# Block products with seven instead of eight multiplications for eight of w_down's 22 tiles

## The chip, the cores and the metric

One core of a Trainium2 chip runs the whole kernel. The metric is device microseconds from launch to end; the median of three runs stands for a kernel. Times below are microseconds (us) unless marked ns. Engines: PE is TensorE, DVE is VectorE, ACT is ScalarE, POOL is GpSimd, SP is SyncE, whose queue issues the loads.

## The reference, cut to what matters

One encoder layer over 512 prompt tokens and 32 sample tokens, 544 in all, with model width 1024 (8 tiles of 128) and hidden width 2816 (22 tiles of 128). It has two feed-forward steps with weights of their own, one ahead of the token mixer and one behind it:

```
g, u = split(rms_norm(r) @ w_gate_up)        # 1024 -> 2 x 2816
h    = silu(g) * u                           # 544 tokens x 2816
y    = h @ w_down                            # 2816 -> 1024
r    = r + 0.5 * rms_norm(y)
```

Behind the first come the mixer (projection, windowed attention and short convolution, projection), behind the second a gate stage ("ple") that ends the layer. All matrices are fp32.

## The kernel before

Every operand of a matmul is split into a high and a low part, `hi` (a rounded copy made by ACT) and `lo` (the rest, source minus hi, made by DVE). A product of two tiles is then three matmuls: hi x hi, hi x lo, lo x hi. Tokens are on the free axis in two halves A and B of 272 (`HT`), so one matmul is 128x128 weights times 128x272. Weights come by SP's queue into four slots of `raw`, are split into `w_split`, and are used.

The stages run in the order up1, down1, mix, out, up2, down2, ple.

**up.** The first `NCL` = 5 hidden tiles are plain products. The other `NJ` = 17 are done in "jobs" of seven block products (the Strassen-Winograd scheme, 2x2 blocks: two halves of the 8 input tiles, gate and up columns, two token halves). A block product is four tiles times three matmuls, 12 matmuls, and a job 84. The order is written out by hand in `SEVEN`: products 1, 2, (3 of the job before), 6, (4 of the job before), 7, 5. In a job DVE makes the block sums (`first_sums`, L1334), POOL two more (L685, L687), ACT the hi parts (`block_hi`, L800), DVE the lo parts (`block_lo`, L1349), and ACT and DVE combine the results (`keep_p1`, `job_c11`, and so on). The split blocks of even and odd jobs have a buffer each.

**down.** `down_group` makes four groups of two output tiles. A group is 2 output tiles x 2 token halves x 22 hidden tiles x 3 matmuls. ACT takes each result out of PSUM (`evacuate`: a square for the norm, then a copy into `y_down`). The hidden tiles are split into `h_hi` and `h_lo` as the last job of up ends (`hidden_hi`, `hidden_lo`). The last group is `last_group`: while PE works on half B, half A's sum of squares (added up by POOL, summed over partitions by a ones-matmul, `all_sums`) is turned into a scale, DVE scales and adds to the residual (`chain_r`), ACT and DVE make the next stage's input (`chain`, `chain_lo`), and the next stage's weights are split (`split_hi`, `split_lo`).

Each engine runs its instructions in the order in which the program issues them; a semaphore wait holds all that is behind it on that engine. At the start of mix, PE asks for the sum of half B's squares (SUM0+2) before the second pair of units (L2178); in ple it asks for it at the seventh of eight input tiles of the first pair:

```
{2: lambda: all_sums(n2 + 1), 6: lambda: all_sums(n2 + 2)}
```

## Time and profile before

| | |
|---|---|
| median of 3 runs | 1053.0 us (1052.49 to 1053.06) |
| span of the profiled execution, first to last instruction | 1051.1 us |
| that execution's own time | not listed; the median is 1.9 us above the span |
| mean granted TensorE clock | 0.996 of full |
| down1 on PE | 260.1 to 393.3 us |
| down2 on PE | 832.3 to 966.6 us |

The times come from the row groups further down. A row of a timeline has the start, the length, the engine and line, output and inputs, how many instructions it merges, and in brackets the idle time before it with what ended it. A matmul's length includes its passage through the array; the next one starts well before it ends, so time per matmul is read from a stretch and its count, not from a length.

### The profile page before, as it was taken

Reading aid. Unit: us, or ns where it says so; the run is one execution under the profiler, and the core shown is the slowest. Engines: PE = TensorE matmul, PEld = TensorE weight load, DVE = VectorE, ACT = ScalarE, POOL = GpSimd, SP = SyncE. Lnnn points to the kernel's source line nnn. Section 1 sums busy time; section 2 is a strip of 40 time slices with the busy share of each in tenths; the row PEclk is TensorE's granted clock in tenths of the full one; section 3 lists DMA queues with packets and bytes.
Section 4 is the critical chain, followed back from the end, with each engine's and each line's share of the span. In section 5 each row is a group of like instructions: output and inputs, shape, how many; then the busy total and the mean of one; then the engine's idle time right before and its main releaser. Section 6 shows DMA issues by size and latency. Waiting matters only on the chain.

```text
span 1051.1 us, 20152 instructions
## 1 busy us (share of the span) xinstructions
PE 1032.0 (98%) x8115; PEld 1015.1 (97%) x8115; DVE 696.1 (66%) x1055; ACT 509.5 (48%) x931; POOL 266.0 (25%) x208
## 2 busy tenths in 40 slices
PE   7999999999999999999999999999999999999997
PEld 7999999999999999998999999999999999999897
DVE  5889777777512259678695898977777741127843
ACT  5555555555522254434455645555555631126664
POOL 3112443431211133000323201343434021113221
PEclk9999999999999999999999999999999999999999
DMA  8314342425333304231224121443333542233102
GB/s 238 94 41 112 91 119 81 121 80 139 102 92 110 80 1 86 80 88 51 70 82 122 41 81 52 112 119 92 110 86 103 147 115 71 83 100 90 34 1 86
DMA packets 182679, 94.77 MB, mean 90 GB/s; under 512 B 11768, under 2 KB 180928, under 8 KB 182592
## 3 DMA queue, kind: packets, MB, share of 16 engines
q1 hardware_dynamic: 182576, 93.56, 32.2%
q8 instruction: 61, 1.00, 0.4%
q14 instruction: 26, 0.21, 0.1%
q10 hardware_dynamic: 16, 0.00, 0.0%
HBM read 91.15 MB, written 2.50 MB: 89 GB/s over the span
## 4 chain that ended last, share of the span: by engine, by line
PE 85%; DVE 9%; ACT 2%; issue 1%; POOL 1%; DMA 1%; SPq 1%; POOLq 0%; DVEq 0%; ACTq 0%
PE bank L1837 14%; PE bank L1835 14%; PE bank L1836 14%; PE bank L1964 9%; PE bank L1967 9%; PE bank L1966 9%; PE bank L1884 5%; PE bank L1892 2%; PE misc L2045 2%; PE misc L1964 1%; PE misc L1967 1%; PE misc L1966 1%; DVE w_split L1242 1%; DVE x_lo L1272 1%; DVE rpre L1248 1%
## 5 line engine op out<-in xcount | busy, mean ns | idle before, releaser
L1837 PE MATMUL bank<-h_hi,w_split 128*128 128x272 f32 x704 | 203.9, 290 | 0.0
L1835 PE MATMUL bank<-h_hi,w_split 128*128 128x272 f32 x704 | 203.0, 288 | 0.0
L1836 PE MATMUL bank<-h_lo,w_split 128*128 128x272 f32 x704 | 202.2, 287 | 0.0
L1242 DVE TENSOR_TENSOR w_split<-raw,w_split 128x1408 fp32r<-128x1408 f32 (+2 forms) x66 | 98.0, 1496 | 146.1 <-ACT w_split L740 146.1
L653 POOL TENSOR_TENSOR ssq<-ssq,sq 128x272 f32<-128x272 f32 x99 | 96.6, 975 | 220.0 <-ACT sq L745 214.3
L1836 PEld LDWEIGHTS bank<-h_lo,w_split 128*128 128x128 f32 x704 | 132.7, 188 | 0.1
L1835 PEld LDWEIGHTS bank<-h_hi,w_split 128*128 128x128 f32 x704 | 132.4, 188 | 0.1
L1837 PEld LDWEIGHTS bank<-h_hi,w_split 128*128 128x128 f32 x704 | 132.3, 188 | 0.0
L1964 PE MATMUL bank<-t_hi,even_blocks 128*128 128x272 f32 x432 | 125.3, 290 | 0.6 <-DVE tU L1367 0.5
L1967 PE MATMUL bank<-t_hi,even_blocks 128*128 128x272 f32 x432 | 125.0, 289 | 0.0
L1966 PE MATMUL bank<-t_lo,even_blocks 128*128 128x272 f32 x432 | 124.4, 288 | 0.0
L740 ACT ACTIVATE w_split<-raw 128x1408 fp32r<-128x1408 f32 (+2 forms) x66 | 80.7, 1242 | 80.7 <-PE bank L1837 74.7
L685 POOL TENSOR_TENSOR s_rest<-s,raw_up 128x512 f32<-128x512 f32 x30 | 66.2, 2207 | 207.6 <-DVE s L1334 207.6
L1964 PE MATMUL bank<-t_hi,odd_blocks 128*128 128x272 f32 x384 | 111.6, 291 | 1.0 <-ACT kept L815 0.8
L1967 PE MATMUL bank<-t_hi,odd_blocks 128*128 128x272 f32 x384 | 111.1, 289 | 0.0
L1966 PE MATMUL bank<-t_lo,odd_blocks 128*128 128x272 f32 x384 | 110.5, 288 | 0.0
L1836 PE MATMUL bank<-x_lo,w_split 128*128 128x272 f32 x320 | 92.1, 288 | 0.0
L1964 PEld LDWEIGHTS bank<-t_hi,even_blocks 128*128 128x128 f32 x432 | 81.3, 188 | 0.9 <-issue 0.9
L1966 PEld LDWEIGHTS bank<-t_lo,even_blocks 128*128 128x128 f32 x432 | 81.4, 188 | 0.0
L1967 PEld LDWEIGHTS bank<-t_hi,even_blocks 128*128 128x128 f32 x432 | 81.3, 188 | 0.0
L1964 PEld LDWEIGHTS bank<-t_hi,odd_blocks 128*128 128x128 f32 x384 | 72.2, 188 | 1.8 <-issue 1.2
L1966 PEld LDWEIGHTS bank<-t_lo,odd_blocks 128*128 128x128 f32 x384 | 72.4, 189 | 0.0
(280 smaller groups left out, 2626.1 us busy)
## 6 DMA issues: line engine op xcount, KB each, us to landing
raw_up<-w_ffn_gate_up SPq DMA_DIRECT2D x88, 512.0 KB, 5.0
raw<-w_ffn_down SPq DMA_DIRECT2D x32, 704.0 KB, 4.8
raw<-w_in SPq DMA_DIRECT2D x14, 512.0 KB, 4.1
raw<-w_ple_gate SPq DMA_DIRECT2D x8, 512.0 KB, 3.8
x_tok<-x_prompt SPq DMA_DIRECT2D x4, 512.0 KB, 5.2
raw<-w_in SPq DMA_DIRECT2D x8, 256.0 KB, 3.8
raw<-w_out SPq DMA_DIRECT2D x16, 128.0 KB, 3.4
raw<-w_out SPq DMA_DIRECT2D x8, 256.0 KB, 3.8
```

What stands on the lines that cost most here:

```text
L653: nc.gpsimd.tensor_tensor(dst, dst, sq[:, s % 2, :], ALU.add).then_inc(summed, 1)
L685: nc.gpsimd.tensor_tensor(s24(j)[:, 0, :], s31[:, 1, :], a[:, 0, :], ALU.add).then_inc(s24_made[n], 1)
L740: nc.scalar.activation(chunk_part(c, 0), chunk_raw(c), ACT.Copy).then_inc(hi_made, 1)
L1242: nc.vector.tensor_tensor(chunk_part(c, 1), chunk_raw(c), chunk_part(c, 0).bitcast(F32), ALU.subtract).then_inc(lo_made, 1)
L1835: nc.tensor.matmul(psum(u), wh, hi, start=(k == 0), stop=False)
L1836: nc.tensor.matmul(psum(u), wh, lo, start=False, stop=False)
L1837: mm = nc.tensor.matmul(psum(u), wl, hi, start=False, stop=(k == n - 1))
L1884: nc.tensor.matmul(psum(u), chunk_part(c, part)[:, k, :], high(k, h), start=(k == 0 and part == 0), stop=False)
L1892: mm = nc.tensor.matmul(psum(u), chunk_part(c, 0)[:, k, :], low(k, h), start=False, stop=(k == KD - 1))
L1964: nc.tensor.matmul(out, hi[:, k, :], x_h, start=(k == 0 and p in (1, 2, 7)), stop=False, skip_group_check=True)
L1966: nc.tensor.matmul(out, hi[:, k, :], x_l, start=False, stop=False, skip_group_check=True)
L1967: mm = nc.tensor.matmul(out, lo[:, k, :], x_h, start=False, stop=(k == 3), skip_group_check=True)
```

## The change

Both down stages are done in three pieces over the 22 hidden tiles.

1. Tiles 0 to 2 (`CA` = 3) by plain products, 16 results of 9 matmuls (`first_tiles`), through three PSUM banks. Their weights (3 tiles x 1024 columns) come in four loads of 384 KB behind product (NJ-2, 4) of the up stage. ACT copies each result to `y_part` (`first_copy`).
2. Tiles 3 to 10 in `NF` = 4 jobs of seven block products (`folded`), each job two output tiles wide, both token halves at once; the 2x2 blocks are two sets of four hidden tiles, two output tiles, two token halves. The token-side blocks are sums of hidden tiles (`fold_sum`, `fold_hi`, `fold_lo`), made once. DVE adds the products into `y_part`: seven adds of 128x272 a job.
3. Tiles 11 to 21 by plain products, 16 results of 33 matmuls; DVE adds `y_part` (`y_add`), then ACT squares from SBUF (`square_y`).

Around them, SP waits for the mixer's cache loads until all of half B's residual is done, the loops of down are written out, and the hidden tiles are split for both halves at once (`hidden_hi`, `hidden_lo`, groups of 3, 2, 2, 2, 2 tiles).

The order and SP's loads of the first tiles:

```diff
-    H_GROUPS = ((0, 2), (14, 18), (2, 4), (4, 6), (6, 10), (10, 14), (18, KF))
+    H_GROUPS = ((11, 14), (14, 16), (16, 18), (18, 20), (20, KF))
...
+    def seven_order(first, last):
+        order = [(j - late, p) for j in range(first, last)
+                 for p, late in ((1, 0), (2, 0), (3, 1), (6, 0), (4, 1), (7, 0), (5, 0)) if j - late >= first]
+        return order[:-2] + [(last - 1, p) for p in (5, 7, 3, 4)]
+    SEVEN, FOLDED = seven_order(0, NJ), seven_order(FOLD0, FOLD0 + NF)
...
+            def load_first_tiles(n, s):
+                sp.wait_ge(product_done[n], nth(NJ - 2, 4))
+                for part in range(4):
+                    cols = slice(part * D // 4, (part + 1) * D // 4)
+                    sp.dma_start(ca_raw[:, :, cols], w_down[s][0:CA * P, cols].rearrange("(k p) c -> p k c", p=P))\
+                        .then_inc(ca_in[part], 16)
```

On ACT, the first tiles, the fold jobs and the squares:

```diff
+            def first_copy(n, v):
+                act.wait_ge(ca_done, 2 * KD * n + v + 1)
+                nc.scalar.activation(y_part(v // 2, v % 2), ca_bank(v), ACT.Copy).then_inc(ca_copied, 1)
...
+            def fold_jobs(n, s, d):
+                after = {0: lambda: first_weights_hi(n, 2), 1: lambda: fold_hi(n, 3), 2: lambda: first_weights_hi(n, 3),
+                         3: lambda: fold_hi(n, 4), 4: lambda: block_hi(n, s, FOLD0, 0), 5: lambda: fold_hi(n, 5),
+                         6: lambda: block_hi(n, s, FOLD0, 1), 8: lambda: fold_hi(n, 6),
+                         10: lambda: block_hi(n, s, FOLD0, 2), 12: lambda: block_hi(n, s, FOLD0, 3)}
+                for v in range(2 * KD):
+                    first_copy(n, v)
+                    if v in after:
+                        after[v]()
+                for j in range(FOLD0 + 1, FOLD0 + NF):
+                    for m in range(4):
+                        block_hi(n, s, j, m)
+                    if j == FOLD0 + 1:
+                        hidden_hi(n, 0)
+                hidden_hi(n, 1)
+                hidden_hi(n, 2)
+                hidden_hi(n, 3)
+                split_hi(C0[d])
                 split_hi(C0[d] + 1)
-                hidden_hi(n, A, 4)
-                job_gate_b(n, NJ - 1)
-            def hidden_hi(n, h, g):
+                hidden_hi(n, 4)
...
+            def square_y(s, i, h, pos):
+                act.wait_ge(y_ready, Y0[s] + 8 * i + 4 * h + pos + 1)
+                square(y_sum(4 * i + pos, h), SQ0[s] + (4 * h if i == 0 else 8 + (4 + KD) * h) + pos).then_inc(squared, 1)
```

On DVE, an add into `y_part`, the end of the up jobs, the fold jobs, and the last output tiles:

```diff
+            def add_p1(n, j):
+                m, i = 2 * (j - FOLD0), j - FOLD0
+                dve.wait_ge(product_done[n], nth(j, 1))
+                dve.wait_ge(ca_copied, 2 * KD * n + 2 * KD)
+                if i:
+                    dve.wait_ge(c11_added, NF * n + i)
+                nc.vector.tensor_tensor(p1_kept_at, chain_bank(j), y_part(m, A), ALU.add).then_inc(p1_added, 1)
...
+                j = NJ - 1
+                job_c22(n, j - 1)
+                job_c11(n, j)
+                fold_sum(n, 1)
+                job_c21(n, j - 1)
+                job_hidden(n, j - 1)
+                job_c22(n, j)
+                first_tiles_lo(n, 1, CA)
+                first_weights_lo(n, 0)
+                fold_sum(n, 2)
+                first_sums(n, s, FOLD0)
+                first_weights_lo(n, 1)
+                job_c21(n, j)
+                job_hidden(n, j)
+                first_weights_lo(n, 2)
+                fold_sum(n, 3)
+                first_weights_lo(n, 3)
+                fold_lo(n, 0), fold_lo(n, 1)
+                block_lo(n, s, FOLD0, 0)
+                fold_lo(n, 2)
+                block_lo(n, s, FOLD0, 1)
+                fold_lo(n, 3)
+                block_lo(n, s, FOLD0, 2), block_lo(n, s, FOLD0, 3)
+                fold_lo(n, 4)
...
+            def fold_jobs(n, s, d):
+                for j in range(FOLD0, FOLD0 + NF - 1):
+                    if j > FOLD0:
+                        add_u4(n, j - 1)
+                        add_c22(n, j - 1)
+                    first_sums(n, s, j + 1)
+                    add_p1(n, j)
+                    block_lo(n, s, j + 1, 0)
+                    add_c11(n, j)
+                    if j > FOLD0:
+                        add_c12(n, j - 1)
+                    block_lo(n, s, j + 1, 1)
+                    add_u2(n, j)
+                    if j > FOLD0:
+                        add_c21(n, j - 1)
                     else:
+                        fold_lo(n, 5), fold_lo(n, 6)
+                    block_lo(n, s, j + 1, 2)
+                    block_lo(n, s, j + 1, 3)
+                    if j > FOLD0:
+                        continue
+                    hidden_lo(n, 0)
+                j = FOLD0 + NF - 1
+                add_u4(n, j - 1)
+                add_c22(n, j - 1)
+                add_p1(n, j)
+                hidden_lo(n, 1)
+                add_c11(n, j)
+                add_c12(n, j - 1)
+                hidden_lo(n, 2)
+                add_u2(n, j)
+                add_c21(n, j - 1)
+                hidden_lo(n, 3)
+                add_u4(n, j)
+                split_lo(C0[d])
+                add_c22(n, j)
                 split_lo(C0[d] + 1)
+                add_c12(n, j)
+                add_c21(n, j)
+                hidden_lo(n, 4)
...
+            def y_add(s, i, h, pos):
+                n, v, m = FFN[s], 8 * i + 4 * h + pos, 4 * i + pos
+                if v == 0:
+                    for added in (c11_added, c12_added, c21_added, c22_added):
+                        dve.wait_ge(added, NF * (n + 1))
+                dve.wait_ge(unit_done, U0[s] + v + 1)
+                nc.vector.tensor_tensor(y_sum(m, h), psum(U0[s] + v), y_part(m, h), ALU.add).then_inc(y_ready, 1)
+            def down_stage(s, ci):
+                c0, c1, with_p = C0[s], C0[s] + KD, s == "down2"
+                split_lo(c0 + 2), split_lo(c0 + 3)
+                for pos in range(4):
+                    y_add(s, 0, A, pos)
+                for pos, j in enumerate((6, 7, 4, 5)):
+                    y_add(s, 0, B, pos)
+                    split_lo(c0 + j)
+                for pos in range(4):
+                    y_add(s, 1, A, pos)
+                chain_r(ci, A, y_sum, SUM0[s], {3: lambda: y_add(s, 1, B, 0), 6: lambda: y_add(s, 1, B, 1)})
+                split_lo(c1), split_lo(c1 + 1)
                 if with_p:
                     p_lo(0)
+                chain_lo(ci, A, range(0, KD // 2))
+                y_add(s, 1, B, 2)
+                split_lo(c1 + 2)
                 if with_p:
                     chain_lo(ci, A, range(KD // 2, KD))
                     p_lo(1), p_lo(2)
+                    y_add(s, 1, B, 3)
                 else:
+                    y_add(s, 1, B, 3)
+                    split_lo(c1 + 3)
                     chain_lo(ci, A, range(KD // 2, KD))
```

On PE, the first tiles and the waits of the fold jobs:

```diff
+            def first_tiles(n):
+                for v in range(2 * KD):
+                    m, h = divmod(v, 2)
+                    if v == 0:
+                        pe.wait_ge(ca_lo_made, 2 * n + 2)
+                    if v % 4 == 0:
+                        pe.wait_ge(ca_w_lo_made, 4 * n + v // 4 + 1)
+                    if v > 2:
+                        pe.wait_ge(ca_copied, 2 * KD * n + v - 2)
+                    cols = slice(m * P, (m + 1) * P)
+                    for k in range(CA):
+                        x_h, x_l = half(ca_hi, k, h), half(h_lo, k, h)
+                        nc.tensor.matmul(ca_bank(v), ca_w_hi[:, k, cols], x_h, start=(k == 0), stop=False)
+                        nc.tensor.matmul(ca_bank(v), ca_w_hi[:, k, cols], x_l, start=False, stop=False)
+                        mm = nc.tensor.matmul(ca_bank(v), ca_w_lo[:, k, cols], x_h, start=False, stop=(k == CA - 1))
+                    mm.then_inc(ca_done, 1)
...
+                    if p == 6:
+                        pe.wait_ge(p1_added, NF * n + i + 1)
+                    if p == 5:
+                        pe.wait_ge(u2_added, NF * n + i + 1)
+                    if p == 3:
+                        pe.wait_ge(u4_added, NF * n + i + 1)
...
+                    if p == 4:
+                        pe.wait_ge(c22_added, NF * n + i + 1)
```

## Rows read from the trace of the kernel before

**Rows 1.** The page: busy time by engine; granted clock in 40 slices.

```profile
PE 1032.0 (98%) x8115; PEld 1015.1 (97%) x8115; DVE 696.1 (66%) x1055; ACT 509.5 (48%) x931; POOL 266.0 (25%) x208
...
PEclk9999999999999999999999999999999999999999
```

**Rows 2.** Windows (busy by engine, clock, DMA): jobs of up1, down1.

```profile
78.70:260.10 181.40, 180.86 (x1431) 180.26 (x1430) 140.46 (x162) 96.94 (x156) 65.43 (x30) 1.00 0.38 105
260.10:393.30 133.20, 133.20 (x1061) 133.12 (x1060) 47.21 (x46) 47.44 (x74) 26.82 (x23) 1.00 0.29 81
```

**Rows 3.** Costliest groups: one of down's three matmul lines.

```profile
L1837 PE MATMUL bank<-h_hi,w_split 128*128 128x272 f32 x704 | 203.9, 290 | 0.0
```

**Rows 4.** Waits of PE, whole span: waiter, releaser, total, times, longest.

```profile
PE bank L1884 <- ACT x_hi_up L758: 3.1, 1, 3.1
...
PE misc L2045 <- ACT out_tok L1192: 1.5, 1, 1.5
...
PE bank L1964 <- DVE tU L1367: 0.5, 1, 0.5
```

**Rows 5.** DVE groups by shape, 78 to 394 us: busy, mean, idle before.

```profile
L1334 DVE TENSOR_TENSOR s<-raw_up 128x1024 f32<-128x1024 f32 x16 | 19.5, 1216 | 0.0
...
L1427 DVE TENSOR_TENSOR h_lo<-h_raw,h_hi 128x1088 fp32r<-128x1088 f32 x8 | 10.1, 1290 | 0.9 <-ACT h_hi L885 0.9
...
L1349 DVE TENSOR_TENSOR even_blocks<-s_rest,even_blocks 128x1024 fp32r<-128x1024 f32 x8 | 9.8, 1219 | 0.5 <-ACT even_blocks L800 0.5
...
L1349 DVE TENSOR_TENSOR even_blocks<-raw_up,even_blocks 128x512 fp32r<-128x512 f32 x9 | 6.2, 685 | 0.0
...
L1367 DVE TENSOR_TENSOR tU<-bank,kept 128x272 f32<-128x272 f32 x9 | 4.0, 439 | 2.9 <-ACT kept L822 2.9
```

**Rows 6.** ACT groups by shape, the same stretch.

```profile
L885 ACT ACTIVATE h_hi<-h_raw 128x1088 fp32r<-128x1088 f32 x8 | 8.6, 1106 | 2.4 <-PE bank L1967 1.5 <-DVE h_raw L1382 1.0
...
L815 ACT ACTIVATE kept<-bank 128x272 f32<-128x272 f32 x17 | 6.8, 397 | 17.3 <-PE bank L1967 17.3
```

**Rows 7.** Timeline of DVE, then POOL, in one up1 job (start, length).

```profile
239.22 1.97 DVE L1349 TENSOR_TENSOR even_blocks<-s,even_blocks 128x1024 fp32r<-128x1024 f32 x1
...
243.31 0.44 DVE L1374 TENSOR_TENSOR tU<-bank,kept 128x272 f32<-128x272 f32 x1 [2.12 <-PE bank L1967]
...
237.89 2.21 POOL L685 TENSOR_TENSOR s_rest<-s,raw_up 128x512 f32<-128x512 f32 x1 [6.15 <-DVE s L1334]
```

**Rows 8.** Window in which three loads of w_down arrive.

```profile
248.00:250.00 2.00, 2.00 (x18) 2.00 (x17) 0.64 (x2) 0.95 (x3) 0.00 (x0) 1.00 1.02 302
```

**Rows 9.** Timeline at the end of down1: DVE, PE, PE.

```profile
388.85 3.51 DVE L1242 TENSOR_TENSOR w_split<-raw,w_split 128x1024 fp32r<-128x1024 f32 x2
...
397.30 1.08 PE L1857 MATMUL misc<-ssq,ones 128*128 128x272 f32 x4
...
409.44 4.53 PE L1884 MATMUL bank<-x_hi_a,w_split 128*128 128x272 f32 x34 [0.66 <-DVE zq L1603]
```

**Rows 10.** Timeline of POOL there: one squares add.

```profile
376.95 0.77 POOL L653 TENSOR_TENSOR ssq<-ssq,sq 128x272 f32<-128x272 f32 x1 [7.55 <-ACT sq L745]
```

**Rows 11.** Timeline at the end of down2: three of DVE, two of PE.

```profile
965.23 2.78 DVE L1272 SCALAR_TENSOR_TENSOR x_lo<-r,gT,x_hi_a 128x272 fp32r<-128x272 f32 x4
...
971.50 1.41 DVE L1503 TENSOR_TENSOR pT_lo<-misc,pT_hi 128x272 fp32r<-128x272 f32 x4
...
976.81 1.86 DVE L1248 RECIPROCAL misc<-misc 128x272 f32<-128x272 f32 x1
...
970.14 0.70 PE L1857 MATMUL misc<-ssq,ones 128*128 128x272 f32 x2
...
984.86 2.77 PE L1884 MATMUL bank<-x_hi_a,w_split 128*128 128x272 f32 x20 [0.26 <-DVE tG L1770]
```

**Rows 12.** PE's timeline, then a window, at the start of the kernel.

```profile
12.50 5.82 PE L1884 MATMUL bank<-x_hi_up,w_up 128*128 128x272 f32 x32 [3.07 <-ACT x_hi_up L758]
...
13.00:14.00 1.00, 1.00 (x7) 1.00 (x6) 1.00 (x3) 1.00 (x4) 0.00 (x0) 0.50 1.22 288
```

More of the change, by code:

```diff
@@ L57, in encoder_layer @@
     NJ = KF - NCL
-    STAGES = [("up1", 2 * KF, 4 * NCL, KD), ("down1", 2 * KD, 2 * KD, MAXK), ("mix", len(MIX), 2 * len(MIX), KD),
-              ("out", KD, 2 * KD, KD), ("up2", 2 * KF, 4 * NCL, KD), ("down2", 2 * KD, 2 * KD, MAXK),
+    CA, NF = 3, KD // 2
+    FOLD0, NJT = NJ + 1, NJ + NF
+    STAGES = [("up1", 2 * KF, 4 * NCL, KD), ("fold1", KD, 0, KD), ("down1", KD, 2 * KD, MAXK),
+              ("mix", len(MIX), 2 * len(MIX), KD), ("out", KD, 2 * KD, KD), ("up2", 2 * KF, 4 * NCL, KD),
+              ("fold2", KD, 0, KD), ("down2", KD, 2 * KD, MAXK),
               ("ple", KD, 4 * KD, KD + KP)]
@@ L127, in encoder_layer @@
              ("norm_ffn2_post", "norm_ple_pre"), ("norm_ple_post", None)]
-    FFN = {"up1": 0, "down1": 0, "up2": 1, "down2": 1}
+    FFN = {"up1": 0, "fold1": 0, "down1": 0, "up2": 1, "fold2": 1, "down2": 1}
+    FOLD = {"up1": "fold1", "up2": "fold2"}
     SQ0 = {"start": 0, "down1": 16, "mix": 48, "out": 64, "down2": 96, "ple": 128}
@@ L407, in encoder_layer @@
               for s, w in (("up1", "w_ffn1_gate_up"), ("up2", "w_ffn2_gate_up"))}
-        down = {s: t[w][0].rearrange("(j k p) (m c) -> m j p k c", j=2, p=P, c=P)
-                for s, w in (("down1", "w_ffn1_down"), ("down2", "w_ffn2_down"))}
+        w_down = {"up1": t["w_ffn1_down"][0], "up2": t["w_ffn2_down"][0]}
+        fold = {s: w[CA * P:(CA + 8) * P, :].rearrange("(k p) (m c) -> m p k c", p=P, c=P) for s, w in w_down.items()}
+        down = {s: w[(CA + 8) * P:FF, :].rearrange("(k p) (m c) -> m p k c", p=P, c=P) for s, w in w_down.items()}
         w_in = t["w_in"][0].rearrange("(k p) n -> p k n", p=P)
@@ L583, in _ @@
             sp.dma_start(x_tok[0:DEC, XT - 1, :], t["x_sample"][0]).then_inc(x_in[XT - 1], 16)
-            for s, d in (("up1", "down1"), ("up2", "down2")):
+            for n, (s, d) in enumerate((("up1", "down1"), ("up2", "down2"))):
                 load_up(s, 2 if s == "up1" else 0, SLOTS)
@@ L862, in jobs @@
                         keep_u4(n, j)
[L863 to L886 removed]
+                    block_hi(n, s, j + 1, 2)
@@ L1383, in job_hidden, with first_tiles_lo, first_weights_lo @@
                                         up_at(j)[:].rearrange("p h t -> p (h t)"), ALU.mult).then_inc(h_job_made[n], 1)
-            def jobs(n, s, d):
-                for j in range(NJ):
-                    more = j + 1 < NJ
+            def first_tiles_lo(n, a, b):
+                dve.wait_ge(ca_hi_made, 2 * n + (2 if a else 1))
+                nc.vector.tensor_tensor(h_lo[:, a:b], h_raw[:, a:b], ca_hi[:, a:b].bitcast(F32), ALU.subtract)\
+                    .then_inc(ca_lo_made, 1)
+            def first_weights_lo(n, part):
+                cols = slice(part * D // 4, (part + 1) * D // 4)
+                dve.wait_ge(ca_w_hi_made, 4 * n + part + 1)
+                nc.vector.tensor_tensor(ca_w_lo[:, :, cols], ca_raw[:, :, cols], ca_w_hi[:, :, cols].bitcast(F32),
+                                        ALU.subtract).then_inc(ca_w_lo_made, 1)
@@ L1389, in jobs, with fold_lo @@
+            def fold_lo(n, b):
+                dve.wait_ge(fold_hi_made, 7 * n + b + 1)
+                if b == 2:
+                    dve.wait_ge(fold_summed, 4 * n + 4)
+                nc.vector.tensor_tensor(fold_low(b), fold_raw(b), t_hi[:, b].bitcast(F32), ALU.subtract)\
+                    .then_inc(fold_lo_made, 1)
+            def jobs(n, s):
+                for j in range(NJ - 1):
                     if j > 1:
                         job_c22(n, j - 1)
-                    if more:
-                        first_sums(n, s, j + 1)
+                    first_sums(n, s, j + 1)
@@ new lines, in down_stage @@
+            def down_stage(s, n, hooks_b):
+                first_tiles(n)
+                folded(n)
+                for v in range(2 * KD):
+                    i, h, pos = v // 8, v % 8 // 4, v % 4
+                    c, hooks = C0[s] + 4 * i + pos, hooks_b.get(pos) if (i, h) == (1, B) else None
+                    if h == A:
+                        pe.wait_ge(lo_made, split_no[c])
+                    if v < 4:
+                        pe.wait_ge(c12_added if v < 2 else c21_added, NF * n + NF - 1 + v % 2)
+                    else:
+                        pe.wait_ge(y_ready, Y0[s] + v - 3)
+                    if v == 0:
+                        hooks = {a - MAXK: lambda g=g: pe.wait_ge(h_lo_made[n], g + 1) for g, (a, _) in enumerate(H_GROUPS)}
+                    product(U0[s] + v, [(c, k - MAXK, h_high(k, h), half(h_lo, k, h)) for k in range(MAXK, KF)], hooks)
```

467 lines of the change are left out of this document (267 added, 200 removed).

## The prediction

> **What bounds the kernel now.** I read the page first: PE is busy for 98% of the span, DVE for 66%, at a granted clock of nine tenths or more throughout [rows 1]. So a matmul that is taken away shortens the kernel, unless another engine makes PE wait in its place. Next the windows: 1061 matmuls in the 133.20 us of down1 is 0.126 us each, and the 17 jobs of up1 (17 x 84 = 1428 matmuls in 181.4 us) come to 0.127 [rows 2]. I use 0.126, which makes a block product (12 matmuls) 1.51 us. Last the waits of PE: hardly any lie in the stages that change; the long ones are 3.1 us at the start of the kernel and 1.5 us in ple [rows 4]. The timelines at the two ends of down show something the shares hide: there DVE, not PE, sets when the next stage can go on. PE waits 0.66 us on DVE at 409.44 and again at 984.86 [rows 9, 11].
>
> **The matmuls.** Before, each of down's three matmul lines has 704 in both stages [rows 3], 2112 in all, 1056 a stage. After: 16 x 9 = 144, 4 x 84 = 336, 16 x 33 = 528, together 1008. That is 48 fewer a stage, 96 in all: 96 x 0.126 = **-12.1 us**. Everything else is a matter of waits.
>
> **Entry to the first tiles.** PE's 0.5 us wait on `job_c22` in up2's last job [rows 4] goes, since that add is no longer behind a split: **-0.5**. New is the wait for the first tiles' weights. Their loads start when product (15, 4) ends, four products or 6.0 us before PE wants them. With three loads on the way the DMA moves 302 GB/s [rows 8], so 0.39 MB is 1.3 us, behind a start-up that I put at 2 to 2.5 us. Then come ACT's copy of 768 elements (about 0.8, between 0.40 for 272 and 1.11 for 1088 [rows 6]) and DVE's difference (about 0.95, between 0.69 for 512 and 1.22 for 1024 [rows 5]). 3.6 + 0.8 + 0.95 = 5.4 fits in 6.0. I take **+0.2** for both stages; if landing takes 5 us it is +1 each.
>
> **The 18.1 us of first tiles.** A result is 9 x 0.126 = 1.13 us and PE may be two results ahead of ACT's copies. Up to the eighth copy ACT has 8 x about 0.33 plus seven larger operations of 0.75 to 1.0 us (ends overlap the next start, so I take a little off the lengths of [rows 6]): about 9.1 us, started 1.6 us into the stage, done at 10.7. PE needs that copy for its eleventh result, at 11.3. So 0, and up to +0.7 a stage. DVE has about 17.5 us of work between the first weights' lo part and the last `fold_lo` (eight operations of 1088 elements at 1.20, three weight parts at 0.9, the block sums and lo parts at 1.14, 1.14, 1.14, 1.14 and 0.65, two adds), and ends about when PE does; the last one is not needed for another 6.0 us. 0.
>
> **The first fold job** has a place where DVE is late. It has only five products, 7.53 us, since products 3 and 4 belong to the next. Call its start on PE F. The first product ends at F + 1.7 with latency; from there DVE must do in order: `add_p1` 0.35, lo part 1.14, `add_c11` 0.35, the lo part beside POOL's sums 1.97, `add_u2` 0.35, two `fold_lo` 2.40, lo parts 1.14 and 0.65, `hidden_lo` of 1632 elements 1.80, `add_u4` 0.35: 10.5 us (lengths of [rows 5, 7], less the 0.08 by which successors overlap). `add_u4` is done at F + 12.2. PE asks for it at product (18, 3), the eighth: F + 7 x 1.507 = F + 10.55. Wait 1.7 us. Behind it DVE's `add_c22` 0.35, `first_sums` 1.14, `add_p1` 0.35 end at F + 14.1, while PE asks at F + 13.8: 0.35 more. After that DVE has an add of 0.35 in place of the 0.78 us hidden product and three adds more, some 0.7 us in a job in which it idles 2.1 us for one wait alone [rows 7]: no further wait. Two stages x 2.05 = **+4.1**. Bounds: 0.7 a stage if the 1.97 is 1.22 and the splits overlap better; 3.3 if the fold splits run into POOL's sums as that one does.
>
> The Trainium skill says in GPSIMD Engine Reference, section Specifications, that POOL and VectorE contend when a VectorE instruction has two SBUF inputs. The trace agrees in part: 1.97 us beside POOL's sum against 1.22 for the same shape without it, while other lo parts are not stretched [rows 5, 7]. If it held for each of them, the fold jobs' wait would be at the upper bound above.
>
> **The last fold job and the plain tiles.** Nothing is late there by the same sums: `add_c22` ends 0.35 us before product (21, 4), and `y_add` has 4.15 us a result. 0.
>
> **End of down1.** The results of half B are now added on DVE instead of copied by ACT, four adds of 0.36 in the queue where PE already waits. `chain_r` ends 0.72 later, 389.6 in the old time frame. Then two splits 3.5 [rows 9], `chain_lo` on four tiles 2.7, `y_add` (B, 2) 0.36, a split 1.14 to 1.75, `y_add` (B, 3) 0.36: about 398.0. ACT squares (0.4), POOL adds (0.77 [rows 10], up to 1.5 beside a split), so PE's sum of half B can run at 399.1 to 400.4. Before it ran from 397.30 [rows 9]. PE waits about 2.2 us. It gets 0.66 of this back at 409.44, where it waited anyway; DVE's own chain is 1.0 to 1.6 later. **+1.6**, between 1.0 and 2.8.
>
> **End of down2** is worse. DVE's queue was: `x_lo` from 965.23, a split, more `x_lo`, `pT_lo`, which ends at 972.9 [rows 11]. The two early adds are absorbed (DVE waited there for ACT), `y_add` (B, 2) costs 0.36, and `y_add` (B, 3) comes after all of them: 973.65. Square 0.4, POOL's add 0.8, latencies: 975.1. PE wants the sum at 970.14 [rows 11]: a wait of 5.0 us. Next the gates: two tiles of hi x hi and the lo pass, 2 us, give DVE gate 0 at 977.8 and gate 1 at 978.8; split 1.4, and the reciprocal that ran from 976.81 starts at 980.6, 3.8 late. PE itself is 5.0 late less 0.35 and 0.26 of old waits, so the matmuls of 984.86 start 4.4 late: **+4.4**, between 3.5 and 5.5.
>
> **The clock there.** At the start of the kernel PE waited 3.07 us, the granted clock fell to 0.50 (1.2 GHz), and the next 32 matmuls took 5.66 us to the next instruction instead of 4.0 [rows 12]. The 1.5 us wait of [rows 4] left it at 2.4 GHz [rows 1]. A wait of 5.0 us is nearer to the first: **+1.5** in down2's end, 0 elsewhere (2.2 is below 3.07); bounds 0 and 1.7 for each of the two ends. [...]
>
> **Sum.** -12.1 - 0.5 + 0.2 + 4.1 + 1.6 + 4.4 + 1.5 = -0.8 us. The span becomes 1051.1 - 0.8 = 1050.3; the median stands 1.9 above the span, so 1052.2; I round to **1052.0**.
>
> **Rivals.**
> - *The late adds cost less.* If PE reaches the two sums later, or the clock holds, the ends cost 3 us instead of 7.5 and the fold jobs 2 instead of 4.1: -12.1 - 0.5 + 0.2 + 2 + 3 = -7.4, 1045.6. For it: all terms but the matmuls rest on DVE's queue being as full as I count it. Against it: the chain of PE on DVE at both ends is in the trace. With a part of it (no clock loss and a better fold job, -3.5) it is 1049.5. Chance 0.35 together, most of it in the nearer part.
> - *DVE becomes the bound at the fold jobs.* If POOL's sums stretch each split beside them, the fold jobs wait 3.3 a stage (+2.5), the first tiles' copies 0.7 (+1.4), and the clock also falls at down1's end (+1.7): already the first is enough with one of the others; from +2.9 over my sum the kernel is slower. All of it gives 1057.8. For it: 1.97 against 1.22 [rows 7, 5]. Against: only one of four lo parts shows it. Chance 0.2.
> - *The weights of the first tiles are late.* +1 to +2 in all, 1053.5; inside no change. It has 0.1 of the chance below.
>
> My forecast with the third rival has the remaining 0.45. 0.2% is 2.1 us, about what a measurement of this kernel can tell: faster is below 1050.9, slower above 1055.1. From the cases: faster 0.36, same 0.44, slower 0.20. The range reaches to the nearer part of the first rival and to the start of the second: 1047.5 to 1055.5.
>
> **What would show it.** PE with 96 matmuls fewer; a wait of about 1.7 us in each fold stage at the eighth product, ended by DVE's add for product 5; a wait of about 2 us ahead of the sums at the start of mix; one of about 5 us at the last sum of half B in ple, released by POOL behind ACT behind DVE, and after it a window with a clock near 0.5. If PE shows no such wait in ple, my order of DVE's queue is wrong and the time is that of the first rival. If ACT is named as the releaser between the first tiles, the copies are late and it is the second.

## The result, and the profile after

| | before | after |
|---|---|---|
| median | 1053.03 us (20 runs) | 1054.64 us (20 runs, 1053.55 to 1055.29) |
| ratio | | 1.0014, 95% interval 1.0007 to 1.002 |
| span of the profiled execution | 1051.1 us | 1051.8 us |
| mean granted clock | 0.996 | 0.994 |
| down1 starts on PE | 260.1 us | 259.7 us |
| mix starts | 393.3 us | 390.2 us |
| wait on `zq` in mix ends | 409.4 us | 407.5 us |
| down2 starts | 832.2 us | 829.5 us |
| ple starts | 966.6 us | 961.3 us |
| output transposes start | 992.9 us | 993.6 us |

The change made the kernel slower by 0.14%: less than the 0.2% that I called no change, and inside the range, but 2.6 us above the forecast and on the other side of the kernel before: I had 1.0 us faster, it is 1.6 slower.

The page of the changed kernel, its first part. It answers to [rows 1]: 96 matmuls fewer, and DVE from 66% to 74%.

```profile
PE 1021.9 (97%) x8019; PEld 1003.8 (95%) x8019; DVE 782.3 (74%) x1183; ACT 532.0 (51%) x955; POOL 285.0 (27%) x224
```

The waits of PE over the whole span, as in [rows 4]: waiter, releaser, total, times, longest.

```profile
PE misc L2127 <- issue: 5.2, 1, 5.2
PE bank L2328 <- DVE kept L1626: 3.0, 2, 1.5
...
PE bank L2328 <- DVE kept L1620: 1.6, 2, 0.8
PE misc L2127 <- POOL ssq L739: 1.5, 1, 1.5
...
PE bank L2328 <- DVE kept L1607: 0.6, 2, 0.3
```

L2127 is `all_sums`: 5.2 us at the last sum of half B in ple, 1.5 at the same sum in mix. L1626 is `add_u4`, L1620 `add_u2`, L1607 `add_p1`, once in each down stage. The waits for `add_u4`, `add_p1` and the two sums are in the prediction, with 1.7, 0.35, 5.0 and 2.2 us. The one for `add_u2` is not. The wait on `tU` (0.5) is gone, as forecast.

TensorE's timeline across the first fold job of down1 (start, length, what it waited for). The first product starts at 277.72.

```profile
283.62 0.29 PE L2331 MATMUL bank<-t_hi,even_blocks 128*128 128x272 f32 x1
284.70 0.36 PE L2328 MATMUL bank<-t_hi,even_blocks 128*128 128x272 f32 x1 [0.80 <-DVE kept L1620]
284.90 0.29 PE L2330 MATMUL bank<-h_lo,even_blocks 128*128 128x272 f32 x1
...
289.16 0.29 PE L2331 MATMUL misc<-t_hi,odd_blocks 128*128 128x272 f32 x1
290.96 0.36 PE L2328 MATMUL bank<-t_hi,even_blocks 128*128 128x272 f32 x1 [1.51 <-DVE kept L1626]
...
292.42 0.29 PE L2331 MATMUL bank<-t_hi,even_blocks 128*128 128x272 f32 x1
292.99 0.36 PE L2328 MATMUL bank<-t_hi,odd_blocks 128*128 128x272 f32 x1 [0.28 <-DVE kept L1607]
```

The starts tell more than the bracket. In a run of matmuls they are 0.126 us apart. Over the three waits they are 1.08, 1.80 and 0.57 apart, and the start behind each is 0.20 further on, not 0.126. So waits listed with 0.80 + 1.51 + 0.28 = 2.6 us cost TensorE's stream of matmuls 0.95 + 1.67 + 0.44 + 3 x 0.07 = 3.3 us. The stage as a whole says the same: 133.2 us before, 130.5 after, and 48 matmuls are 6.05, so 3.4 us went elsewhere. The second stage gives 134.4 and 131.8, 3.4 again.

DVE's timeline in that job, then POOL's. They answer to [rows 7].

```profile
278.31 1.21 DVE L1456 TENSOR_TENSOR s<-raw_up 128x1024 f32<-128x1024 f32 x1
279.44 0.42 DVE L1607 TENSOR_TENSOR kept<-bank,y_low 128x272 f32<-128x272 f32 x1
279.79 2.17 DVE L1471 TENSOR_TENSOR odd_blocks<-raw_up,odd_blocks 128x1024 fp32r<-128x1024 f32 x1
281.89 0.43 DVE L1614 TENSOR_TENSOR y_low<-misc,kept 128x272 f32<-128x272 f32 x1
282.24 1.96 DVE L1471 TENSOR_TENSOR odd_blocks<-s,odd_blocks 128x1024 fp32r<-128x1024 f32 x1
284.13 0.43 DVE L1620 TENSOR_TENSOR kept<-bank,y_low 128x272 f32<-128x272 f32 x1
```

```profile
279.59 1.29 POOL L766 TENSOR_TENSOR s_rest<-s,raw_up 128x512 f32<-128x512 f32 x1 [14.12 <-DVE s L1456]
280.97 2.15 POOL L768 TENSOR_TENSOR s_rest<-s_rest,raw_up 128x512 f32<-128x512 f32 x1
```

Two lo parts are stretched beside POOL's sums, not one: 2.17 and 1.96 against 1.21 alone. And POOL's first sum is the quick one here, 1.29, where it took 2.21 in [rows 7].

The ends of these rows show how the two engines share the time: they take turns. POOL's first sum ends at 280.88, and the lo part that started during it ends 1.08 later, at 281.96. POOL's second sum started during that lo part and ends 1.16 after it, at 283.12. The second lo part started during that sum and ends 1.08 after it, at 284.20. So 2.17, 2.15 and 1.96 are each a wait for the other engine's instruction and then the operation's own time.

The end of down2: PE, then DVE, then windows (length; busy time and count of PE, PEld, DVE, ACT, POOL; granted clock; DMA share; GB/s). They answer to [rows 11, 12].

```profile
970.21 1.24 PE L2127 MATMUL misc<-ssq,ones 128*128 128x272 f32 x2 [5.23 <-issue]
970.87 2.40 PE L2154 MATMUL bank<-x_hi_b,w_split 128*128 128x272 f32 x8
```

```profile
967.07 1.40 DVE L1767 TENSOR_TENSOR pT_lo<-misc,pT_hi 128x272 fp32r<-128x272 f32 x4
968.39 0.42 DVE L1777 TENSOR_TENSOR y_down<-bank,y_high 128x272 f32<-128x272 f32 x1
```

```profile
968.00:970.20 2.20, 0.00 (x0) 0.02 (x1) 1.35 (x4) 0.78 (x2) 0.76 (x1) 0.50 0.23 63
...
972.20:973.20 1.00, 1.00 (x6) 1.00 (x6) 0.00 (x0) 1.00 (x1) 0.00 (x0) 0.50 0.00 0
...
974.20:975.20 1.00, 1.00 (x10) 1.00 (x9) 0.41 (x1) 0.00 (x0) 0.00 (x0) 1.00 0.00 0
```

`y_add` (B, 3), L1777, stands behind `pT_lo` and is done at 968.8. ACT's square and POOL's add follow it, and the sum runs at 970.21. The name "issue" in the row hides this chain: PE stood behind several semaphores, and the last is POOL's. While PE stands, the granted clock falls to 0.50, which is 1.2 GHz, and it is back at 1.00 (2.4 GHz) in the last window. What the low clock costs is read from the starts (a window's count also takes in matmuls that only reach into it): from the eight matmuls to the group behind them it is 2.20 us here (970.87 to 973.07). In the kernel before it was 1.21, 970.47 to 971.68, with this row:

```profile
970.47 1.37 PE L1884 MATMUL bank<-x_hi_b,w_split 128*128 128x272 f32 x8
```

### The profile page after: what moved, and what is told of

Read it like the earlier page. It is cut to its first block, busy times and chain, and to the rows that moved or that the text cites. A ratio compares the mean times of both kernels' runs of the same rounds, so it can differ in the third digit from the quotient of the medians.

```text
span 1051.8 us, 20086 instructions
## 1 busy us (share of the span) xinstructions
PE 1021.9 (97%) x8019; PEld 1003.8 (95%) x8019; DVE 782.3 (74%) x1183; ACT 532.0 (51%) x955; POOL 285.0 (27%) x224
## 4 chain that ended last, share of the span: by engine, by line
PE 85%; DVE 10%; issue 2%; ACT 1%; DMA 1%; SPq 1%; POOL 0%; POOLq 0%; DVEq 0%; ACTq 0%
PE bank L2105 11%; PE bank L2106 11%; PE bank L2107 11%; PE bank L2234 9%; PE bank L2236 9%; PE bank L2237 9%; PE bank L2154 5%; PE bank L2162 2%; PE bank L2328 2%; PE bank L2331 2%; PE bank L2330 2%; PE misc L2352 2%; PE misc L2236 1%; PE misc L2234 1%; PE misc L2237 1%
## 5 line engine op out<-in xcount | busy, mean ns | idle before, releaser
L766 POOL TENSOR_TENSOR s_rest<-s,raw_up 128x512 f32<-128x512 f32 x38 | 77.9, 2049 | 304.9 <-DVE s L1456 304.9
L739 POOL TENSOR_TENSOR ssq<-ssq,sq 128x272 f32<-128x272 f32 x99 | 93.0, 939 | 127.0 <-ACT sq L828 121.4
L768 POOL TENSOR_TENSOR s_rest<-s_rest,raw_up 128x512 f32<-128x512 f32 x38 | 80.9, 2130 | 3.0
L1364 DVE TENSOR_TENSOR w_split<-raw,w_split 128x1024 fp32r<-128x1024 f32 (+2 forms) x46 | 66.2, 1455 | 16.6 <-ACT w_split L823 16.6
L2106 PE MATMUL bank<-h_lo,w_split 128*128 128x272 f32 x264 | 76.1, 288 | 0.0
L2234 PEld LDWEIGHTS bank<-t_hi,odd_blocks 128*128 128x128 f32 x384 | 72.3, 188 | 1.7 <-issue 1.1
L2237 PEld LDWEIGHTS bank<-t_hi,odd_blocks 128*128 128x128 f32 x384 | 72.3, 188 | 0.0
L823 ACT ACTIVATE w_split<-raw 128x1024 fp32r<-128x1024 f32 (+2 forms) x46 | 53.1, 1181 | 37.7 <-PE bank L2107 29.1
L2105 PE MATMUL bank<-x_hi_a,w_split 128*128 128x272 f32 x240 | 70.7, 294 | 0.6 <-DVE w_split L1364 0.6
L2107 PE MATMUL bank<-x_hi_a,w_split 128*128 128x272 f32 x240 | 69.2, 288 | 0.0
L2106 PEld LDWEIGHTS bank<-x_lo,w_split 128*128 128x128 f32 x320 | 60.3, 188 | 0.0
```

The lines of the kernel that those rows point to most:

```text
L739: nc.gpsimd.tensor_tensor(dst, dst, sq[:, s % 2, :], ALU.add).then_inc(summed, 1)
L766: nc.gpsimd.tensor_tensor(s24(j)[:, 0, :], s31[:, 1, :], a[:, 0, :], ALU.add).then_inc(s24_made[n], 1)
L768: nc.gpsimd.tensor_tensor(s24(j)[:, 1, :], s24(j)[:, 0, :], a[:, 1, :], ALU.add).then_inc(s24_made[n], 1)
L823: nc.scalar.activation(chunk_part(c, 0), chunk_raw(c), ACT.Copy).then_inc(hi_made, 1)
L1364: nc.vector.tensor_tensor(chunk_part(c, 1), chunk_raw(c), chunk_part(c, 0).bitcast(F32), ALU.subtract).then_inc(lo_made, 1)
L2105: nc.tensor.matmul(psum(u), wh, hi, start=(k == 0), stop=False)
```

## The experiments

All times are medians; the changed kernel is 1054.6, the kernel before 1053.0 (1052.9 to 1053.05 in its executions beside the experiments). The own time of a profiled execution is 1.74 to 1.84 us above its span wherever it is on record.

### 1. The last add ahead of the lo parts (ple_add_early)

```
 if with_p:
-    chain_lo(ci, A, range(KD // 2, KD))
-    p_lo(1), p_lo(2)
     y_add(s, 1, B, 3)
+    chain_lo(ci, A, range(KD // 2, KD))
+    p_lo(1), p_lo(2)
```

> Against the changed kernel (1054.6): the last y_add of down2 stands right behind the split of the third weight tile, ahead of the rest of x_lo and pT_lo. Theory (DVE's queue order makes PE wait 5.2 us for the last sum in ple, and the idle time costs the clock about 1.5 us more): the wait falls to 1 to 1.5 us, the granted clock stays at full after it, and the time falls by 4.5 to 6 us, to 1049 to 1050. Rival (the sum is held by POOL's backlog or by ACT, not by DVE's order): the wait stays above 4 us and the time moves by less than 1 us. Rival (DVE's own chain ends last anyway, so PE's wait is hidden): the wait goes but comes back at PE's next wait on DVE, and the time moves by less than 2 us.

Measured: 1049.7 us, ratio 0.9968 (0.9956 to 0.998); 4.9 us less than the changed kernel. PE's timeline in ple, then windows:

```profile
967.48 0.70 PE L2127 MATMUL misc<-ssq,ones 128*128 128x272 f32 x2 [2.05 <-issue]
967.81 1.37 PE L2154 MATMUL bank<-x_hi_b,w_split 128*128 128x272 f32 x8
969.02 2.14 PE L2162 MATMUL bank<-x_lo,w_split 128*128 128x272 f32 x16
```

```profile
966.00:968.00 2.00, 0.52 (x3) 0.49 (x3) 2.00 (x4) 0.60 (x2) 1.10 (x2) 1.00 0.61 177
```

The wait is 3.2 us shorter (I had expected 1 to 1.5 us to be left; 2.05 are), the clock stays at 1.00, and the eight matmuls take 1.37 us instead of 2.40. From the start of ple to the output transposes it is 27.7 us, 4.5 less than in the changed kernel and 1.4 more than in the kernel before. So the order of DVE's queue is most of what the end of down2 costs.

### 2. The mixer's last sum later (mix_sum_late)

```
-second={0: lambda: (all_sums(n0 + 1), all_sums(n0 + 2))}
+second={0: lambda: all_sums(n0 + 1), 6: lambda: all_sums(n0 + 2)}
```

> Against the changed kernel (1054.6): PE asks for half B's sum in mix six tiles later. Theory (behind down1 DVE's chain sets the start of half B's matmuls, so PE's 1.5 us wait in front of the sum is only in the place of a later one): the 1.5 us wait goes, the wait on DVE near 407.5 grows from 0.66 to about 2 us, and the time changes by less than 0.5 us. Rival (PE's wait is a loss by itself): 1.2 to 1.5 us faster.

Measured: 1054.47 us, ratio 1.001 (1.0001 to 1.0019): 0.2 less than the changed kernel, within its scatter. The waits of PE in mix are now:

```profile
396.81 3.04 PE L2154 MATMUL bank<-x_hi_a,w_split 128*128 128x272 f32 x22 [0.66 <-DVE w_split L1364]
406.83 1.30 PE L2154 MATMUL bank<-x_hi_a,w_split 128*128 128x272 f32 x6 [0.29 <-ACT x_hi_a L841]
408.79 3.40 PE L2154 MATMUL bank<-x_hi_a,w_split 128*128 128x272 f32 x25 [0.65 <-DVE zq L1873]
```

The 1.5 us wait on POOL is gone. The wait on `zq` did not grow to 2 us, as I had expected; two smaller ones, on DVE and on ACT, stand ahead of it. The stretch from the start of mix to the end of the wait on `zq` is 17.55 us, against 17.35 in the changed kernel. So asking later for this sum gains nothing. That fits a chain through DVE that sets the time, with the wait at the start of mix as the first place where its lateness shows; no run made that chain earlier at this end.

### 3. The hidden chunk's lo part out of the first fold job (hidden_late)

```
-if j > FOLD0:
+if j < FOLD0 + 2:
     continue
 hidden_lo(n, 0)
```

> Against the changed kernel (1054.6): the first hidden_lo (1632 elements, 1.8 us) is moved from the end of DVE's first fold job to the end of the third. Theory (DVE is over-full only in the first fold job): PE's wait of 1.5 us on add_u4 and of 0.3 us on the next add_p1 go, the one of 0.8 us on add_u2 stays, and nothing new comes in the later jobs; 2 x 1.8 = 3.6 us faster, 1051.0. Rival (DVE is the bound through all fold jobs): the wait moves to a later fold job, less than 1 us faster.

Measured: 1050.92 us, ratio 0.998 (0.9971 to 0.9989); 3.7 less than the changed kernel. The waits of PE, whole span:

```profile
PE bank L2328 <- DVE kept L1620: 1.6, 2, 0.8
...
PE bank L2328 <- DVE kept L1607: 0.5, 2, 0.3
```

The wait for `add_u4` is gone in both stages and the two others are untouched. By the starts of the matmuls it was 1.67 + 0.07 us a stage, 3.5 in both, near the 3.7 measured. The 1.8 us of hidden work has room in the third fold job.

### 4. TensorE kept busy ahead of the sum in ple (ple_turns)

```
 def all_sums(n, size=None):
+    if n == SUM0["down2"] + 2:
+        pe.wait_ge(inverted, ...)
+        pe.wait_ge(p_ready, 1)
+        for _ in range(36):
+            nc.tensor.transpose(misc[:, 1, 384:512], ones[:], ident[:])
     pe.wait_ge(summed, SUMMED[n])
```

> Against the changed kernel (1054.6): PE makes 36 transposes of ones that nobody reads (about 4.6 us) in its wait for the last sum in ple, and nothing else changes. Theory (the wait also costs the clock): the sum comes at the same time, the granted clock stays at full behind it, and the time falls by about 1.5 us, to 1053.1. Rival (the clock is not what is lost, or DVE hides it): within 0.4 us of 1054.6.

Measured: 1052.41 us, ratio 0.9993 (0.9984 to 1.0002); 2.2 less than the changed kernel, though it does more. PE's timeline:

```profile
965.37 4.09 PE L2118 MATMUL misc<-ident,ones 128*128 128x128 f32 x36
970.72 0.73 PE L2132 MATMUL misc<-ssq,ones 128*128 128x272 f32 x2 [1.26 <-POOL ssq L739]
971.08 1.36 PE L2159 MATMUL bank<-x_hi_b,w_split 128*128 128x272 f32 x8
```

PE gets its sum no sooner, and now the releaser is named: POOL. The eight matmuls take 1.36 us, not 2.40. So the clock alone is worth about 2 us of the 6 at this end: 2.2 by the medians, and 1.8 by the traces, in which the stretch from the start of ple to the output transposes is 30.5 us instead of 32.2. My term for it was 1.5, with a bound of 1.7: the size was a little low.

### 5. The lo part ahead of `add_p1` (lo_before_p1)

```
 first_sums(n, s, j + 1)
-add_p1(n, j)
 block_lo(n, s, j + 1, 0)
+add_p1(n, j)
```

> Edit: in the fold jobs VectorE makes the first lo part of the next job's blocks ahead of add_p1 instead of behind it. In the changed kernel's trace the first fold job's lo parts took 2.17 and 1.96 us beside GpSimd's sums of 1.29 and 2.15, where the kernel before showed 1.22 for a lo part and 2.21 for the sum beside it. Theory: the one that starts first keeps its pace and the other is stretched; add_p1 between the first sums and the lo part lets GpSimd start first. Then the first lo part takes about 1.2 us here and GpSimd's first sum about 2.2, TensorE's wait for add_u2 falls from 0.8 to at most 0.2 us a stage, a wait of some 0.3 for add_p1 may come in front of product 6, and the kernel is 1 to 2 us faster than the changed one (about 1053). Rival: the lo part is stretched wherever it meets GpSimd, whoever starts first; then the lo parts stay at 2 us, the wait only moves, and the time stays within 0.5 us of 1054.6.

Measured: 1055.01 us, ratio 1.0017 (1.0008 to 1.0026). DVE, then POOL, in the first fold job, and the waits of PE there and in the next job:

```profile
280.17 1.21 DVE L1471 TENSOR_TENSOR odd_blocks<-raw_up,odd_blocks 128x1024 fp32r<-128x1024 f32 x1
281.31 0.42 DVE L1607 TENSOR_TENSOR kept<-bank,y_low 128x272 f32<-128x272 f32 x1
...
282.19 1.41 DVE L1471 TENSOR_TENSOR odd_blocks<-s,odd_blocks 128x1024 fp32r<-128x1024 f32 x1
```

```profile
280.32 2.20 POOL L766 TENSOR_TENSOR s_rest<-s,raw_up 128x512 f32<-128x512 f32 x1 [14.12 <-DVE s L1456]
```

```profile
281.88 0.36 PE L2328 MATMUL bank<-t_hi,even_blocks 128*128 128x272 f32 x1 [0.28 <-DVE kept L1607]
291.10 0.36 PE L2328 MATMUL bank<-t_hi,even_blocks 128*128 128x272 f32 x1 [1.46 <-DVE kept L1626]
294.27 0.36 PE L2328 MATMUL bank<-t_hi,odd_blocks 128*128 128x272 f32 x1 [1.41 <-DVE kept L1607]
```

The mechanism is shown. The lo part that starts 0.15 us ahead of POOL takes 1.21 us and POOL's sum 2.20. In the changed kernel POOL started 0.20 ahead, and it was 2.17 and 1.29. The second lo part again ends 1.08 us after POOL's sum (283.60 and 282.52), but since it met only the end of that sum it takes 1.41. The wait for `add_u2` is gone, and the new 0.28 at product 6 is there. The time that I expected of it is not: in the second fold job `add_p1` is now behind a lo part too, and its wait went from 0.28 to 1.41. The waits listed come to 3.15 us a stage instead of 2.6. I had followed the edit through one job only.

### 6. Product 7 twice (product_7_twice)

```
-for k in range(4):
+for k in (*range(4), *range(4)) if p == 7 else range(4):
```

> Edit: in each fold job product 7's twelve matmuls run twice, with the same result: 96 matmuls more, as many as the change took away. At 0.126 us each they are worth 12.1 us if all of TensorE's time is at that pace. Theory: the waits for VectorE in each stage (0.8 for add_u2, 1.5 for add_u4, 0.3 for add_p1) come because the products are short beside VectorE's list; 1.5 us more per product 7 covers the waits for add_u4 and add_p1, which stand behind the first fold job's product 7, but not that for add_u2, which comes ahead of it. Then the time rises by 12.1 less 2 x (1.5 + 0.3) = 8.5 us, to 1063.1. Rival: TensorE's waits are set by something that moves with it (the sums' times are relative to its products), and the time rises by the full 12.1, to 1066.7.

Measured: 1063.46 us, ratio 1.0098 (1.0082 to 1.0113): 8.8 us above the changed kernel for 96 matmuls more, against 12.1 at full price. Two waits are left in down1:

```profile
291.76 0.36 PE L2328 MATMUL bank<-t_hi,even_blocks 128*128 128x272 f32 x1 [1.06 <-DVE kept L1626]
293.79 0.36 PE L2328 MATMUL bank<-t_hi,odd_blocks 128*128 128x272 f32 x1 [0.28 <-DVE kept L1607]
```

The rival, the full 12.1, falls. Of the 12.1 us added at this place 3.3, about a quarter, do not show in the time; by the starts of the matmuls 3.0 of them are waits for DVE that gave way. That removed matmuls pay the same share is not shown, since this adds only to product 7 and takes none away. Which waits give way I had wrong: it is the whole of `add_u2`'s, since product 7 stands ahead of it, and 0.45 of `add_u4`'s, none of `add_p1`'s. So it is luck that the expected 1063.1 was only 0.4 us off.

### 7. Second sums on VectorE (sums_on_dve)

On top of experiment 3, in the second fold job's blocks (the semaphore counts of `second_sums` change with it and are not shown):

```
 # POOL, weight_sums
-if j == 1:
+if j in (1, FOLD0 + 1):
     continue
 # DVE, fold_jobs, first fold job
 add_u2(n, j)
+second_sums(n, s, j + 1)
```

> Edit on top of the kernel without the hidden chunk's lo part in the first fold jobs (1050.9): the two second sums of the second fold job's blocks are made by VectorE behind add_u2, and no longer by GpSimd beside the lo parts. Theory: the lo parts at 2.17 and 1.96 us are stretched by GpSimd; without it each takes some 1.2 us, add_u2 comes 1.7 us sooner and TensorE's 0.8 us wait for it goes, in both stages: 1.6 us less, if the later sums hold up nothing (they come some 2 us later for ScalarE's splits, and VectorE has two operations more). So 1049.3 to 1050.9. Rival: the lo parts are this long for another reason (their own data or ScalarE's splits beside them): they stay at 2 us, the wait stays, and VectorE's two operations more cost up to 1 us a stage: 1051 to 1053.

Measured: 1050.03 us (1049.21 to 1051.4), ratio 0.9972 (0.9961 to 0.9983), against 1050.92 (1050.43 to 1051.35) of experiment 3. DVE's timeline:

```profile
280.61 1.22 DVE L1471 TENSOR_TENSOR odd_blocks<-raw_up,odd_blocks 128x1024 fp32r<-128x1024 f32 x1
...
282.09 1.22 DVE L1471 TENSOR_TENSOR odd_blocks<-s,odd_blocks 128x1024 fp32r<-128x1024 f32 x1
```

Without POOL both lo parts take 1.22 us, and PE no longer waits for `add_u2`. It waits 0.4 for `add_u4` instead, since DVE has 1.3 us more to do. That the stretch comes from POOL is shown. The gain of 1.6 us that I expected is not there; the 0.9 us measured is within the scatter of these two kernels, and experiment 10 does not confirm it.

### 8. Experiments 1 and 3 together (both)

> The two edits tried before, together: y_add of the last group ahead of the lo parts at the end of the second down stage (-4.9 us by itself), and the hidden chunk's first lo part out of the first fold jobs (-3.7 by itself). They lie at different ends of the stages. Theory: they touch different waits and add up: 1054.6 - 4.9 - 3.7 = 1046.0, with TensorE's waits of 5.2 and 1.5 us both gone. Rival: one part of them was the same time seen twice (the hidden lo part that the first edit moves has its end at the same place), and the sum is 1 to 3 us less than that: 1047 to 1049.

Measured: 1047.2 us (1045.85 to 1047.48), ratio 0.994 (0.9926 to 0.9954). The edits alone add up to 1046.0. In ple:

```profile
964.02 0.70 PE L2127 MATMUL misc<-ssq,ones 128*128 128x272 f32 x2 [2.04 <-issue]
964.36 2.01 PE L2154 MATMUL bank<-x_hi_b,w_split 128*128 128x272 f32 x8
966.16 3.08 PE L2162 MATMUL bank<-x_lo,w_split 128*128 128x272 f32 x16
```

```profile
965.00:966.00 1.00, 1.00 (x7) 1.00 (x6) 1.00 (x4) 0.98 (x2) 0.00 (x0) 0.50 0.59 168
```

The same wait as in experiment 1 (2.04 and 2.05 us), but this time the clock fell. The 24 matmuls behind it take 1.6 us more (2.01 + 3.08 against 1.37 + 2.14).

### 9. Both, with 14 transposes in that wait (both_turns)

> With the two edits together TensorE stood idle 2.04 us ahead of its last sum and the granted clock fell to 0.50 (from 964.8 to 968.1 us), though it had stayed at 1.00 over an idle time of 2.05 us at the same place with the first edit alone: the 24 matmuls behind it took 2.01 and 3.08 us instead of 1.37 and 2.14, 1.6 us more. Edit: both edits, and 14 transposes of a constant tile, whose result nothing reads, into that idle time (some 1.5 us of it). Theory: this clock is why the two edits came to 1047.2 and not 1046.0; with TensorE kept busy the clock stays at 1.00 and the time is 1.6 us less, 1045.6. Rival: the two edits overlap somewhere else, TensorE's stretch is hidden behind the reciprocal and the table load that follow, and the time stays within 0.5 us of 1047.2.

Measured: 1046.06 us (1045.24 to 1046.27), ratio 0.9936 (0.9923 to 0.995); 1.1 us less, where I had expected 1.6. In the traces the stretch from the start of ple to the output transposes is 27.7 us instead of 28.9, so 1.2 us less; the spans differ by 1.9 (1043.5 and 1045.4), but 0.8 of that stands ahead of down1, where both run the same code. With the clock held, the sum of the two edits alone (1046.0) is met.

```profile
961.06 1.69 PE L2118 MATMUL misc<-ident,ones 128*128 128x128 f32 x14
963.23 0.73 PE L2132 MATMUL misc<-ssq,ones 128*128 128x272 f32 x2 [0.47 <-POOL ssq L739]
963.59 1.37 PE L2159 MATMUL bank<-x_hi_b,w_split 128*128 128x272 f32 x8
```

### 10. All of them (four_edits)

Experiment 9 with the edit of experiment 7.

> All edits that paid: y_add of the last group first, the hidden lo part late, the 14 transposes, and VectorE making the second fold job's second sums behind add_u2 (0.9 us less on top of the hidden lo part alone). If the last adds to the others: 0.9 us under both_turns, 1044.7 if that one is at 1045.6. Rival: the waits that it removes come back at the next add, and the two kernels are within 0.4 us of each other.

Measured: 1046.05 us (1044.8 to 1046.08), ratio 0.9935 (0.9921 to 0.9949): the same as experiment 9. It beats both kernels, by 6.8 us and 8.6 us, but the second sums on VectorE have no part in that.

## Why the prediction was wrong

My sum against the two profiled executions, in us:

| term | forecast | measured |
|---|---|---|
| 96 matmuls | -12.1 | -12.1 |
| entries of the two stages | -0.3 | -1.1 |
| waits within the two stages | +4.1 | +6.8 |
| end of down1 | +1.6 | +1.2 |
| end of down2, with the clock | +5.9 | +6.0 |
| span | -0.8 | +0.7 |

The measured terms are differences of the landmarks above: 0.4 and 0.7 us at the entries, 3.4 a stage, 390.2 to 407.5 against 393.3 to 409.4 at the end of down1, 961.3 to 993.6 against 966.6 to 992.9 at that of down2. The matmuls' term is their number at 0.126.

**The step that failed** is the sum over DVE's queue in the first fold job, which gave waits of 2.05 us a stage, where 3.4 were lost. In the two stages that is 2.7 us too little. Three things were wrong in it:

- I gave the first lo part 1.14 and only the second 1.97. That first lo part held the queue for 2.10 us (279.79 to 281.89), 0.96 longer; the others were a little quicker than I had them, and the whole list down to `add_u4` took 11.3 us instead of 10.5. I read [rows 7] as "only one of four lo parts shows it", a property of that operation. It is a property of order. In the up job the lo part followed the first sums at once: it began at 237.73, 0.16 ahead of POOL, and took 1.22, and POOL paid with 2.21. In the fold job `add_p1` stands between them; POOL starts first, and DVE pays. And the 1.97 that I took from [rows 7] was no length of its own: that lo part started during POOL's second sum. Experiment 5 turned it round by swapping two instructions, experiment 7 removed it by taking POOL away.
- I priced PE's request for `add_u4` and left out the one for `add_u2`, three products earlier. By my own numbers that add was in time by 0.2 us, too little to pass over; with the late lo part it is a wait of 0.8. Once PE has stood there, its later requests come later too. So `add_u4`'s wait did not grow with the late lo part: 1.5, where I had 1.7. For the same reason the request that I left out cost the sum nothing by itself: what PE loses up to `add_u4` is set by when DVE has made that add.
- I let PE go on at the moment at which the add ends. The matmul starts 0.14 to 0.15 us behind that end, and the next start is 0.07 late. That put some 0.4 us a stage on the two waits that I had priced.

The upper bound that I gave, 3.3 us a stage, was nearly the true value, and part of its condition (the splits run into POOL's sums) had come true in a form that I had not thought of. That the number fits is partly luck: of the 1.2 to 1.35 us a stage above my sum, 0.8 comes from the longer queue and the rest mostly from how a wait ends. It was the price of my second rival, which I gave 0.2. The start of it, 2.9 us over my sum, was not quite reached. That the total was only 2.6 us off is luck in part too, since the entries and the end of down1 gave 1.2 us back.

The Trainium skill says in GPSIMD Engine Reference, section Specifications, that POOL and VectorE contend on instructions of VectorE with two SBUF inputs. The runs agree with more of it than I granted: both lo parts beside POOL's sums were stretched, and the add that reads PSUM between them was not (0.43 beside a sum of 2.15).

**The entries** gave 1.1 instead of 0.3. The first tiles' weights were not late, so that the +0.2 and the third rival fall: in down1 the first of them had landed when ACT copied them at 257.05, 3.2 us after SP's issue at 253.83, and DVE's difference was done at 259.38, 0.3 ahead of PE. The rest is the wait on `tU`, which I had at 0.5 for up2 alone. By the starts of the matmuls it cost 0.7 us there:

```profile
830.59 0.36 PE L1964 MATMUL bank<-t_hi,even_blocks 128*128 128x272 f32 x1 [0.45 <-DVE tU L1367]
```

Up1 had the same wait, too short for the list: at 258.50 a start came 0.39 us after the one before it, and the next 0.20 after that, 0.3 us in all. In the changed kernel neither gap is there.

**Within the stages** nothing else was late: between the first tiles and the first fold job PE doesn't wait, and in the last eleven tiles neither, as forecast. The items of DVE's work in the first tiles add up to 18.2 us, not to the 17.5 that I wrote, but this changes nothing: the last `fold_lo` ended 0.7 us after the first product began, and nothing waited for it.

**The end of down1** cost 1.2, with a wait of 1.5 us instead of 2.2. Experiment 2 fits the reason given for it, that DVE's chain is late: a later request for the sum changes nothing.

**The end of down2** is right in its order and its sum (5.2 for 5.0). Experiments 1 and 4 split it: behind the wait of 5.2 us the low clock costs some 2 us more. The first rival, late adds that cost less, fell: at both ends PE asked for the sums where I had it ask, and in ple the clock did not hold.

**The remaining 1.1 us** of the 2.6 us between forecast and median (the table has 1.5 of them): the profiled execution of the changed kernel took 1053.55, the quickest of its 20; that of the kernel before, by its span, some 1052.9, close to its median. So 0.9 us of the distance between the medians is not in this pair of traces, and 0.2 is my rounding. The profiles of the later kernels put some of this scatter ahead of the change: all run the changed kernel's code up to down1, which starts between 259.4 and 260.6 us in them.

Undoing one stage alone was not tried, nor an earlier add at the end of down1 like that of experiment 1, and neither was a kernel in which POOL's sums are moved to another place in the fold job without giving them to DVE.

## What to carry to other kernels

Price a change that trades matmuls for vector adds by walking through the vector engine's queue, instruction by instruction, and compare each result with the moment at which TensorE asks for it; a result that is in time by only some tenths of a microsecond becomes a wait as soon as one item ahead of it is longer than priced. Two edits to that queue's order, which add no instruction, made of a loss of 1.6 us a gain of 5.8 (1053.05 to 1047.2): put the operation that another engine waits for ahead of those that have time. And when an edit reorders a loop body, follow it through two passes of the loop.
